# Token-tile pipelining at four stage boundaries of a two-block transformer kernel

## What is computed

```
f = (silu(n1(h) @ w_gate1) * (n1(h) @ w_up1)) @ w_down1          # 1024 -> 2816 -> 1024
h = h + 0.5 * rms_norm(f, ffn1_norm_post)
u = rms_norm(h, mix_norm_pre);  m = mixer(u)                     # w_in, attention, LRU, w_out
h = h + rms_norm(m, mix_norm_post)
h = h + 0.5 * rms_norm(swiglu(rms_norm(h, ffn2_norm_pre), ...), ffn2_norm_post)
rms_norm(x, g) = x * rsqrt(mean(x*x) + 1e-6) * g                 # mean over the 1024 features
```

## Time and profile before

| | us |
|---|---|
| runs | 2724.22, 2724.48, 2719.98 |
| median | 2724.22 |
| the profiled execution, its own time | 2720.59 |
| its span | 2718.7 |
| PE busy | 2420.0 (89%) |
| DVE busy | 896.1 (33%) |
| ACT busy | 615.5 (23%) |
| POOL busy | 610.0 (22%) |
| mean granted TensorE clock | 0.935 of full |

### The profile page before, as it was taken

How to read it: one execution, slowest core, us unless ns; L and a number is a source line. 1 busy time by engine, 2 the same in 40 slices (tenths; PEclk the granted TensorE clock), 3 DMA queues, 4 the chain that set the end, 5 groups by cost and what they waited for, 6 DMA issues and landing times.

```text
span 2718.7 us, 30356 instructions
## 1 busy us (share of the span) xinstructions
PE 2420.0 (89%) x12189; PEld 1878.1 (69%) x12190; DVE 896.1 (33%) x1312; ACT 615.5 (23%) x940; POOL 610.0 (22%) x216
## 2 busy tenths in 40 slices
PE   7998789967589999995999994999999795899997
PEld 5644568844449999954888783888866662688785
DVE  4265544432610110124223106132635914322302
ACT  2123323321110000003222114233333303122211
POOL 0023023200100000003444332333413401344431
PEclk7998789988699999997999997999999998899998
DMA  8122400002017888711232212223313221222221
GB/s 271 62 78 71 146 32 1 1 1 95 5 42 263 288 297 294 247 47 31 93 93 93 93 70 79 93 78 109 109 55 116 78 85 47 62 93 93 93 93 70
DMA packets 219925, 276.40 MB, mean 102 GB/s; under 512 B 9655, under 2 KB 199059, under 8 KB 219828
## 3 DMA queue, kind: packets, MB, share of 16 engines
q1 hardware_dynamic: 211744, 267.49, 29.8%
q0 software_dynamic: 1376, 4.26, 0.5%
q10 hardware_dynamic: 6708, 3.29, 0.5%
HBM read 270.79 MB, written 4.24 MB: 101 GB/s over the span
## 4 chain that ended last, share of the span: by engine, by line
PE 86%; DVE 6%; DVEq 3%; ACT 2%; issue 2%; DMA 1%; ACTq 1%; POOL 0%; POOLq 0%
PE bank L2153 42%; PE bank L1831 9%; PE bank L1839 4%; PE bank L635 3%; PE bank L1628 2%; PE bank L603 2%; PE bank L1521 2%; PE bank L2919 2%; PE bank L2040 2%; PE bank L1311 1%; PE bank L433 1%; PE bank L2801 1%; PE bank L1304 1%; PE bank L2820 1%; DVEq L2229 1%
## 5 line engine op out<-in xcount | busy, mean ns | idle before, releaser
L2153 PE MATMUL bank<-hT_high_split,ring_split 128*128 128x512 f32 x2496 | 798.6, 399 | 64.1 <-DVEq L2229 45.8
L2153 PEld LDWEIGHTS bank<-hT_high_split,ring_split 128*128 128x128 f32 x2496 | 472.1, 189 | 177.2 <-DVEq L2229 46.3
L2137 POOL TENSOR_TENSOR ring_split<-ring,ring_split 128x2048 fp32r<-128x2048 f32 x66 | 306.5, 4646 | 1059.9 <-ACT ring_split L2132 1059.9
L2153 PE MATMUL bank<-hT_split,ring_split 128*128 128x512 f32 x1248 | 493.7, 396 | 0.0
L2132 ACT ACTIVATE ring_split<-ring 128x2048 fp32r<-128x2048 f32 x104 | 198.9, 1915 | 700.6 <-DMA ring<-in_ffn_w_up 226.7
L2153 PEld LDWEIGHTS bank<-hT_split,ring_split 128*128 128x128 f32 x1248 | 235.8, 189 | 57.0 <-issue 0.2
L2377 POOL TENSOR_TENSOR ring_split<-ring,ring_split 128x2048 fp32r<-128x2048 f32 x38 | 186.1, 4900 | 361.7 <-ACT ring_split L2132 361.7
L1831 PE MATMUL bank<-arena,ring 128*128 x2048 | 235.9, 276 | 5.5 <-issue 5.5
L1831 PEld LDWEIGHTS bank<-arena,ring 128*128 128x128 f32 x2048 | 233.2, 193 | 5.7 <-issue 5.7
L2153 PE MATMUL bank<-ring_split,hid_high_split 128*128 128x512 f32 x704 | 225.2, 401 | 7.2 <-DVE hid_low_split L2239 7.2
L2153 PEld LDWEIGHTS bank<-ring_split,hid_high_split 128*128 128x128 f32 x704 | 134.6, 191 | 40.9 <-DVE hid_low_split L2239 8.1
(11 more groups left out here) (414 smaller groups left out, 2785.6 us busy)
## 6 DMA issues: line engine op xcount, KB each, us to landing
ring<-in_w_in SPq DMA_DIRECT2D x45, 1024.0 KB, 5.1
ring<-in_w_gate SPq DMA_DIRECT2D x32, 1024.0 KB, 5.5
ring<-in_w_up SPq DMA_DIRECT2D x32, 1024.0 KB, 8.0
ring<-in_w_down SPq DMA_DIRECT2D x32, 1024.0 KB, 7.5
ring<-in_ffn_w_gate SPq DMA_DIRECT2D x22, 1024.0 KB, 5.4
ring<-in_ffn_w_up SPq DMA_DIRECT2D x22, 1024.0 KB, 5.3
ring<-in_ffn_w_down SPq DMA_DIRECT2D x22, 1024.0 KB, 4.9
ring<-in_w_ada SPq DMA_DIRECT2D x16, 1024.0 KB, 5.2
```

Of the source, the lines that this page charges most:

```text
L2137: pool.tensor_tensor(low(n), raw(n), high(n).bitcast(F32), ALU.subtract)\
L2153: mm = pe.matmul(dst, left[l], right[r], start=start and n == 0, stop=stop and n == 2)
```

## The change

The last two down slots of each ffn, and the last two of `w_out_2`, are taken together, tile by tile. PE raises `tile_done` after tiles 0 to 2, and `slots_used` by 2 after tile 3. ACT and DVE norm a tile while PE works on the next ones. The factor and the gain of the next norm are applied on the rows of `X` (gain row `pre`, loaded beside `post`), so nothing is left to scale after the transposes. Tile t is turned into its own two banks (`pe_xT`), ACT copies them straight into `hT_hi`, and DVE forms `hT_lo` from the bank and `hT_hi`. The transposes of tiles 0 and 1 stand in PE's order behind tiles 2 and 3 of the product. ACT splits slot 0 of the next stage inside the boundary, after the root of tile 0; SP may load it while the last pair of slots is in use. Before `ffn1`, ACT splits two slots at the end of the expert stage, and POOL no longer waits at the last `meet`. One more gain row is loaded ahead of the second norm of the first block.

```diff
 # pe_ffn (pe_out2 alike, with the last 2 of 4 slots and one product each)
-            for i in range(NPAIRS):
+            for i in range(NPAIRS - 2):
...
                 mm.then_inc(S("slots_used"), 1)
+            w = [down(NPAIRS - 2), down(NPAIRS - 1)]
+            for t in range(NT):
+                for half in range(2):
+                    for i in range(2):
+                        for kk_ in range(2):
+                            mm = add(w[i], NPAIRS - 2 + i, kk_, t, half)
+                if t < NT - 1:
+                    mm.then_inc(S("tile_done"), 1)
+                else:
+                    mm.then_inc(S("slots_used"), 2)
+                if tag == "ffn1" and t >= 2:
+                    pe_xT(pe, t - 2)
+
+        def pe_xT(pe, t):
+            nxt(pe, "xn_ready")
+            for k in range(KD):
+                mm = pe.transpose(bank[2 * t + k // 4][:, (k % 4) * P:(k % 4 + 1) * P], f_xn[t % 2][:, k, :], ident)
+            mm.then_inc(S("x_turned"), 1)
...
+        def act_post(act, t, last):
+            if t < NT - 1:
+                nxt(act, "tile_done")
+            else:
+                act.wait_ge(S("slots_used"), last)
+            for half in range(2):
+                act.activation(split_at(junkf_all, 3, half), turned_of(t, half), ACT.Square,
+                               accum_out=f_ss[:, t, half:half + 1])
+            act.drain().then_inc(S("f_squares"), 1)
+            nxt(act, "f_ss")
+            act.activation(f_r[:, 1, t:t + 1], f_r[:, 0, t:t + 1], ACT.Sqrt, bias=eps, scale=1.0 / D)\
+               .then_inc(S("f_root"), 1)
...
+        def act_xT(act, t):
+            nxt(act, "x_turned")
+            for half in range(2):
+                i = act.activation(split_at(hT_hi, t, half), turned_of(t, half), ACT.Copy)
+            i.then_inc(S("xT_high"), 1)
+
+        def act_between(act, last, next_tag):
+            for t in range(NT):
+                act_post(act, t, last)
+                if t == 0:
+                    act_high(act, next_tag, 0)
+                nxt(act, "x_new")
+                act_rms(act, t)
                 if t:
-                    root(t - 1)
...
+                    act_xT(act, t - 1)
+            act_xT(act, NT - 1)
...
+        def dve_post_scale(dve, t):
+            nxt(dve, "f_squares")
+            dve.tensor_tensor(f_r[:, 0, t:t + 1], f_ss[:, t, 0:1], f_ss[:, t, 1:2], ALU.add).then_inc(S("f_ss"), 1)
+            dve.drain()
+            for half in range(2):
+                c = slice(512 * half, 512 * half + 512)
+                dve.tensor_tensor(f_tmp[:, c], bank[2 * t + half][:, :], post[:, c], ALU.mult)
+            nxt(dve, "f_root")
+            dve.reciprocal(f_r[:, 0, t:t + 1], f_r[:, 1, t:t + 1])
+            dve.drain()
+            dve.scalar_tensor_tensor(X[:, t, :], f_tmp, f_r[:, 0, t:t + 1], X[:, t, :], ALU.mult, ALU.add)\
+               .then_inc(S("x_new"), 1)
+
+        def dve_unit(dve, t):
+            nxt(dve, "rms_ready")
+            dve.reciprocal(ss[:, t:t + 1], rstd[:, t:t + 1])
+            dve.drain()
+            dve.scalar_tensor_tensor(f_xn[t % 2], X[:, t, :].rearrange("p (k n) -> p k n", k=KD), ss[:, t:t + 1],
+                                     pre.rearrange("p (k n) -> p k n", k=KD), ALU.mult, ALU.mult)\
+               .then_inc(S("xn_ready"), 1)
+
+        def dve_xT(dve, t):
+            nxt(dve, "xT_high")
+            for half in range(2):
+                i = dve.tensor_tensor(split_at(hT_lo, t, half), turned_of(t, half),
+                                      split_at(hT_hi, t, half).bitcast(F32), ALU.subtract)
+            i.then_inc(S("hT_low"), 1)
...
+        def dve_between(dve, factor):
+            dve_post_row(dve, factor, 2)
+            for t in range(NT):
+                if t:
+                    dve_unit(dve, t - 1)
+                if t >= 2:
+                    dve_xT(dve, t - 2)
+                dve_post_scale(dve, t)
+            dve_unit(dve, NT - 1)
+            for t in (NT - 2, NT - 1):
+                dve_xT(dve, t)
+            dve.drain()
...
 # sp_mix; sp_ffn of ffn2 alike
-                sp.wait_ge(S("slots_used"), MIX + max(n - 2, 0))
+                sp.wait_ge(S("slots_used"), MIX + n - 2)
```

More of the change, by code:

```diff
@@ L2246, in dve_ffn, with act_rows_in @@
                 unit(u, ROUNDS)
-        def act_gain(act, name, after=None):
+        def act_rows_in(act, post_name, pre_name, after=None):
             if after is not None:
                 act.wait_ge(S("slots_used"), after)
-            act.dma_start(post, a[name][0:1, :].broadcast_to([P, D])).then_inc(S("post_loaded"), 16)
-        def act_post(act, last):
-            def root(t):
-                nxt(act, "f_ss")
-                act.activation(f_r[:, 1, t:t + 1], f_r[:, 0, t:t + 1], ACT.Sqrt, bias=eps, scale=1.0 / D)\
-                   .then_inc(S("f_root"), 1)
-            act.wait_ge(S("slots_used"), last)
-            for t in range(NT):
-                for half in range(2):
-                    act.activation(f_sq[:, half, :], bank[2 * t + half][:, :], ACT.Square,
-                                   accum_out=f_ss[:, t, half:half + 1])
-                act.drain().then_inc(S("f_squares"), 1)
-                if t:
-                    root(t - 1)
-            root(NT - 1)
@@ L2270, in dve_post, with turned_of @@
-        def dve_post(dve, factor):
-            def total(t):
-                nxt(dve, "f_squares")
-                dve.tensor_tensor(f_r[:, 0, t:t + 1], f_ss[:, t, 0:1], f_ss[:, t, 1:2], ALU.add).then_inc(S("f_ss"), 1)
-            nxt(dve, "post_loaded", 16)
+            for dst, name in ((post, post_name), (pre, pre_name)):
+                if name is not None:
+                    act.dma_start(dst, a[name][0:1, :].broadcast_to([P, D])).then_inc(S("post_loaded"), 16)
+        def turned_of(t, half):
+            return bank[2 * t + half][:, :].rearrange("p (k n) -> p k n", n=P)
@@ L2291, in dve_post, with dve_norm1, dve_last @@
+        def dve_norm1(dve):
+            nxt(dve, "post_loaded", 16)
+            for t in range(NT):
+                dve_unit(dve, t)
+                if t:
+                    dve_xT(dve, t - 1)
+            dve_xT(dve, NT - 1)
+            dve.drain()
+        def dve_last(dve, factor):
+            dve_post_row(dve, factor, 1)
+            for t in range(NT):
+                dve_post_scale(dve, t)
             dve.drain()
@@ L2538, in act_mix @@
         def act_mix(act):
-            for n in range(2):
-                mix_high(act, n)
+            mix_high(act, 1)
             act_coefficients(act)
@@ L2911, in pe_out2, with add @@
             nxt(pe, "m_attn", KD - 2)
-            for i in range(4):
+            def add(w, i, kk_, t, half):
+                k = 2 * i + kk_
+                return pe.matmul(bank[2 * t + half][:, :], merged[:, k, t * P:(t + 1) * P],
+                                 w[:, kk_, 512 * half:512 * half + 512], start=(k == 0), stop=(k == KD - 1))
+            for i in range(2):
                 w = mix_raw(pe, OUT2 + i)
@@ L2915, in pe_out2 @@
                 for kk_ in range(2):
[L2916 removed]
                     for t in range(NT):
                         for half in range(2):
[L2919 to L2920 removed]
+                            mm = add(w, i, kk_, t, half)
                 mm.then_inc(S("slots_used"), 1)
+            w = [mix_raw(pe, OUT2 + i) for i in (2, 3)]
+            nxt(pe, "m_merged", 2)
+            for t in range(NT):
+                for half in range(2):
+                    for i in range(2):
+                        for kk_ in range(2):
+                            mm = add(w[i], 2 + i, kk_, t, half)
+                if t < NT - 1:
+                    mm.then_inc(S("tile_done"), 1)
+                else:
+                    mm.then_inc(S("slots_used"), 2)
+                if t >= 2:
+                    pe_xT(pe, t - 2)
         def sp_out(sp):
```

155 lines of the change are left out of this document (69 added, 86 removed).

## The result

The changed kernel takes **2647.27 us** (median of 4 executions, 2646.24 to 2648.04). The kernel before, run beside it on the same chip, takes 2724.35 (2719.98 to 2727.11). The ratio is 0.9718, 95% interval 0.9701 to 0.9735: 77 us saved. The profiled execution took 2647.43 us (span 2645.6), the one of before 2720.6 (2718.7): 73.2 us between the two traces, to be set beside the forecast sum of 68.7.

The account below looks back on a forecast made before the run. PE's idle time at four boundaries, together 138.3 us, was taken to set the end. 16.2 + 22.2 + 19.6 + 11.7 - 0.6 - 0.4 = 68.7 us saved, 2651.9 for the profiled execution, forecast 2655 us as median, range 2643 to 2670.

Parts of the forecast that it names:

- Before `ffn1`: Boundary from the experts' last products to ffn1: hole of 35.6 us, PE to start 16.2 us earlier.
- From `ffn1` to `mix`: First middle boundary: PE to start mix 41.7 us after the last pair's start instead of 63.9, gain 22.2 us.
- the hold of 3.1 us at tile 0: Middle boundaries: DVE's unit step on tile 0 reads SBUF alone and waits for POOL's subtraction, 3.1 us.
- No hold: Rival, middle boundaries: POOL starts late or yields, so DVE's unit step is not held; 2649 us, chance 0.13.
- From `mix` to `ffn2`: Second middle boundary, same chain: PE to start 39.5 us after the pair's start instead of 59.1, gain 19.6 us.
- The end: After PE's last product: the last tile's chain takes 4.3 us instead of 16.0, gain 11.7 us.
- The stall at the pair's start: Last pair of each ffn waits for POOL's low part of slot 32: 0.3 us lost each, 0.6 in all.
- The added row: Gain row issued on ACT's queue ahead of the first block's second norm: 0.37 us, 0.4 us on the path.
- the rival that it stays low: PE's clock stays at the 1.2 GHz level after the boundaries' small transpose clusters: 2745 us, chance 0.03.
- The table load: ACT's table load charged 1.28 us once in each boundary, without the skill's extra drain of some 1.38 us.
- The strided writes: Strided half-tile writes of 128 columns in three boundaries: nothing charged, at most 11 us by a factor of 1.5.
- A longer relay: Rival: strided forms cost up to 11 us, or mix starts with a second POOL hold, 5; 2660 to 2666, chance 0.2.

Follow-up runs that it names:

- Experiments 3 and 4: Edits of the kernel after: 3 splits slot 0 only behind the boundary's last copies, 2656.03 us; 4 starts POOL's subtraction after DVE's last unit step, 2646.09 us.
- experiment 1: The added gain row for the norm before ffn1 issued behind the routing, nothing else differing from the kernel after: 2639.71 us, ratio 0.9701 to the kernel before.

## Why the prediction was right, and where not

The verdict, the direction and the range held: 2655 was forecast with 2643 to 2670, and 2647.3 measured. The mechanism held in three of the four boundaries; that the total came so near is in part luck, as the last paragraph of this section adds up. By parts:

- **Before `ffn1`**: 16.2 us forecast, 14.8 measured. The transposes of tiles 0 and 3 cost 1.94 and 1.97 us, not the 5.84/4 = 1.46 of four tiles in a row. They ran at a granted clock of 0.50, the old 32 at 0.62 on the average; those of tile 2, behind a wait too but at 1.00, took 1.09. This lies on the path at tile 0 and again at tile 3, and makes 1.0 of the 1.4.
- **From `ffn1` to `mix`**: 41.7 us after the pair's start was forecast, 41.3 measured. Each term is in the trace: the hold of 3.1 us at tile 0 (4.11 less 1.28 is 2.8), the relay of 7.3 us a tile (7.18), two groups of transposes amid products at 0.9 (1.03). Experiments 3 and 4 show the hold to be POOL's. *No hold*, the first rival, is out.
- **From `mix` to `ffn2`**: 19.6 us forecast, 30.3 measured, the largest miss and **the mis-sized term**. "One tile of `w_out_2`'s last pair is 8 at 55.19/128 = 0.431: 3.45 us" took one pass for each product. The row says x128 for the 64 calls of the stage: each is two instructions, so the tile is 16 of them, 6.9 us, and the pair 27.6 instead of 13.8. The trace agrees: the stage starts at 2191.43, and the transposes behind three of the four tiles of the pair start at 2239.57, 48.1 us on, against 27.6 + 3 x 6.9 = 48.3. With 6.9 the old boundary is 27.6 + 45.3 = 72.9 us, and the new one was measured at 42.6, where 39.5 was forecast; the pair that covers the relay is twice as long as I took it to be. The forecast wait of 4 us before tile 3 never came.
- **The end**: 11.7 us forecast and measured, 4.3 us from the last product to the last addition.
- **The stall at the pair's start**: 0.3 us forecast in each ffn, 0.45 and 0.47 seen. It is POOL's, as said.
- **The added row**: 0.4 us forecast, 5.8 lost, 7.3 won back by experiment 1. The row's own cost is about 7.1 (4.6 and 2.5); the profiled execution of the kernel after came to its first issue on this queue 1.2 us sooner than that of the kernel before (661.83 against 663.01), which hides a part. The step that failed is the choice of the row for its price: 0.37 us was the issue of the same kind at a quiet time (1606.53), and this one stands right behind two others while the DMA fills the ring with the experts' weights. A row of the kernel before would have told it, the timeline of SP's DMA queue at the same time:

```profile
655.69 4.01 SPq L1794 DMA_DIRECT2D ring<-in_w_up  x1
659.74 3.87 SPq L1799 DMA_DIRECT2D ring<-in_w_down  x1
```

  An issue took 4 us there, ten times the plain one. The cost that comes after it, products at the low clock, was not thought of at all.
- **Not in the sum**: 2.4 us before `w_out_2` (4.3 from the port, less 1.7 in the 64 products of line 2880, 27.7 us instead of 29.4; in other traces of these kernels they take either), and 2.7 us won in `ffn2`. The 2.7 are not the change's work but that execution's: in the second trace of the kernel after `ffn2` takes 379.9 us, in the eleven traces with the changed boundaries 375.4 to 379.9. Most of it, 2.2 us, is an even difference of pace over the first two thirds of the stage, at full clock in both. Stretches of 100 us in `ffn2`, 80 us behind its start, of the kernel before, the kernel after and its second trace (columns of the earlier trace rows):

```profile
2400.00:2500.00 100.00, 100.00 (x430) 80.43 (x430) 25.20 (x26) 26.14 (x21) 41.04 (x10) 1.00 0.30 94
...
2341.24:2441.24 100.00, 100.00 (x435) 81.12 (x434) 26.69 (x26) 26.12 (x21) 41.80 (x10) 1.00 0.30 94
...
2344.35:2444.35 100.00, 100.00 (x430) 80.47 (x429) 25.32 (x26) 26.15 (x21) 41.10 (x10) 1.00 0.30 94
```

  What sets the pace is open.
- **The clock**: the rival that it stays low (2745) is out. Stretches of the kernel after, with the first 6 us of `ffn2` in the kernel before at the end (us, PE, PEld, DVE, ACT, POOL busy, granted clock, DMA, GB/s):

```profile
1631.00:1645.90 14.90, 3.94 (x16) 3.14 (x16) 9.40 (x16) 7.70 (x18) 0.00 (x0) 0.54 0.42 135
1645.90:1652.00 6.10, 6.09 (x20) 4.86 (x21) 3.13 (x2) 4.88 (x4) 4.44 (x1) 0.73 0.54 134
1652.00:1670.00 18.00, 18.00 (x79) 14.51 (x78) 8.96 (x19) 3.00 (x3) 8.71 (x3) 1.00 0.18 58
...
2261.60:2267.60 6.00, 6.00 (x15) 4.73 (x16) 0.00 (x0) 3.34 (x3) 5.78 (x2) 0.55 0.00 0
...
2320.36:2326.36 6.00, 6.00 (x15) 4.70 (x16) 0.00 (x0) 0.00 (x0) 0.00 (x0) 0.52 0.00 0
```

  The clock is back at the 2.4 GHz level within some 6 us of each boundary, as before. What the shorter holes change there is small and goes both ways: the granted clock of the first 6 us behind the boundary is 0.67 against 0.76 before in `ffn1`, 0.73 against 0.64 in `mix`, and 0.55 against 0.52 in `ffn2`. The first 20 products take 0.5 us more, 0.5 less and 0.2 less.

- **The table load**: 1.28 us at 1611.88, and the root at 1613.17, in the kernel after as well. The Trainium skill ("ScalarE: Activation LUTs", What ACT_TABLE_LOAD costs) adds some 1.38 us of drain to each switch; by that `mix` would have started at about 43 us after the pair's start, and it started at 41.3. The row decides.
- **The strided writes**: nothing was charged, up to 11 us were kept as a bound. They cost nothing: 1.28 us for two instructions of line 2335, and 1.28 for line 2328 with the strided buffer (`hT`) as with the plain one. *A longer relay*, the second rival, is out, though its other half was near: the small steps of DVE at the start of `mix` are held by POOL (3.15 us for eight elements at 1649.04), which no product of PE waited for.

The sum, 68.7 us, came within 4.5 us of the trace, 73.2, and that is luck: the misses lay on both sides. 10.7 and 2.7 us more were won at `w_out_2` and in `ffn2`, and 5.4, 2.4 and 1.4 us were lost or not won at the row, before `w_out_2` and before `ffn1`. Of these the 2.7, the 2.4 and 1.2 us of the row's stretch vary from execution to execution. The other 3.2 us of the 7.7 by which the median was missed come from going on from the trace to the median: the kernel before was profiled in a quick execution, 3.6 us below its median, and I added most of that to the forecast, while the profiled execution of the kernel after lies at its median.

## What to carry to other kernels

Count the instructions of a row against the calls in the code before you make a unit of it; a float32 product may be two. The price of issuing a DMA is that of its moment: an issue that is behind others while the transfers are full goes on a queue that nothing waits for, or later. When a boundary between stages becomes a relay of tiles, its pitch is the sum of what the two engines hand each other in series, so order each engine's work on a tile so that the step the other one waits for comes first (7.2 us a tile became 6.0 before `mix`). Where a third engine keeps one of the two out, let it begin when its result is needed (2.6 us before `mix`; nothing before `ffn2`, where PE's own tiles set the pace). And before a difference of a few us in one stage is put down to a change, look at the same stage in a second trace of the same kernel.

## What the hardware did that was not expected

- **The issue of a DMA on ACT's queue took 4.64 us** (4.6 to 4.9 in all eight traces with this order) where the same kind takes 0.33 to 0.45 elsewhere.
- **The port between DVE and POOL is won for a whole instruction, but who gets it in a row of instructions is not told by who comes first.** The Trainium skill ("SBUF — State Buffer", SBUF: two separate sides) has it as an exclusive lock that goes to whoever starts first, for the whole instruction. The trace agrees for one instruction (4.11 us of DVE beside 4.62 of POOL). With eight instructions of DVE back to back, POOL got in once after 3.2 us (9.22 and 4.83) and once not until all sixteen were through (4.91 and 10.78). What decides between the two is open. It is not how long after DVE's first product POOL starts, as far as the traces resolve it: POOL got in with 3.23 to 3.43 us (seven traces) and was kept out with 3.24 to 3.39 (four).
- **Even tiny instructions of DVE are held**: a tensor_scalar over 128 x 8 took 3.15 us and a product over 128 x 8 took 4.22 beside POOL (1649.04 and 1652.54 in the kernel after, POOL from 1647.56 to 1656.74), while a reciprocal of one column took its usual 0.16 in the midst of a subtraction (1616.72, POOL from 1615.36 to 1619.98).
- **Executions of one kernel are 2 to 11 us apart.** When line 2257 is first issued, traces of kernels that are the same up to there already differ by up to 8.1 us (658.1 to 666.2 over the eight traces with that order). Later three stretches that no edit touches take one of two lengths: 27.7 or 29.4 us for the products of line 2880, 13.7 to 13.9 or 18.0 to 18.3 us of wait for `rec_ready`, and 231.1 or 233.3 ns a product over the first thousand products of an ffn (the quicker in three of the 24 ffn stages on record). What makes them was not tried.
